# Neighbourhood attention's values with tokens on the partitions, gathered by transfers within SBUF

## The reference, cut to what matters

```python
qa, ka, va, cq, ckv, kr, gates = jnp.split(h @ w_in, IN_SPLITS, axis=-1)
...
v_b = jnp.moveaxis(lax.dynamic_slice_in_dim(vg, rs, kh, axis=1)[:, :, key_col], 2, 1)
...
p = jax.nn.softmax(jnp.concatenate([s_loc, s_ctx], axis=-1), axis=-1).astype(v.dtype)
p_loc = p[..., :n_loc].reshape(B, H, n_blk, NA_QCOLS, kh, NA_KCOLS)
o = (jnp.einsum('bhjqak,bjakhd->bjqhd', p_loc, v_b)
     + jnp.einsum('bhjqk,bkhd->bjqhd', p[..., n_loc:], v_ctx))
```

## Time and profile before

| | before |
|---|---|
| runs shown | 2722.70, 2722.75, 2722.99 us |
| median | 2722.75 us |
| span of the profiled execution | 2720.7 us |
| TensorE busy | 2686.7 us, 99% |
| VectorE, ScalarE, GpSimd busy | 1318.2, 514.4, 822.1 us |
| stretch of the change: end of the rope product to first scores | 816.28 to 823.75 us |

### The profile page before, as it was taken

How to read it: one execution, slowest core, us unless ns; L and a number is a source line. 1 busy time by engine, 2 the same in 40 slices (tenths; PEclk the granted TensorE clock), 3 DMA queues, 4 the chain that set the end, 5 groups by cost and what they waited for, 6 DMA issues and landing times.

```text
span 2720.7 us, 30606 instructions
## 1 busy us (share of the span) xinstructions
PE 2686.7 (99%) x12154; PEld 2037.8 (75%) x12154; DVE 1318.2 (48%) x2572; ACT 514.4 (19%) x1185; POOL 822.1 (30%) x682
## 2 busy tenths in 40 slices
PE   9999999999999999999999999999999999999998
PEld 3655555556886478888888887885578888888887
DVE  7656555577227564334332346217563325544433
ACT  3100000004117361122000102106430011000012
POOL 0433343241313004402443430220044404444420
PEclk9999999999999999999999999999999999999999
DMA  6334333223200102222222221220012222222220
GB/s 259 128 112 139 105 112 124 89 87 126 93 26 17 55 1 78 86 78 83 88 94 79 92 93 62 78 80 32 32 62 84 87 78 93 89 82 93 79 99 31
DMA packets 56926, 231.72 MB, mean 85 GB/s; under 512 B 4432, under 2 KB 16592, under 8 KB 43472
## 3 DMA queue, kind: packets, MB, share of 16 engines
q1 hardware_dynamic: 46112, 194.07, 20.3%
q0 software_dynamic: 8352, 31.46, 3.8%
q10 hardware_dynamic: 2320, 4.24, 0.4%
HBM read 227.66 MB, written 2.10 MB: 84 GB/s over the span
## 4 chain that ended last, share of the span: by engine, by line
PE 61%; DVE 1%; ACT 0%; issue 0%; DVEq 0%; ACTq 0%
PE banks L760 40%; PE banks L675 13%; PE banks L753 2%; PE banks L811 1%; PE banks L1468 1%; PE banks L1387 1%; PE banks L1405 1%; PE banks L922 0%; PE banks L1470 0%; PE banks L1462 0%; PE banks L1315 0%; PE banks L1476 0%; PE banks L1446 0%; PE banks L726 0%; PE banks L727 0%; PE banks L1295 0%
## 5 line engine op out<-in xcount | busy, mean ns | idle before, releaser
L3165 POOL TENSOR_TENSOR big<-weight_ring 128x512 f32<-128x512 f32 (+2 forms) x121 | 146.3, 1209 | 1292.3 <-PE banks L760 674.5
L760 PE MATMUL banks<-big 128*128 128x256 f32 (+1 forms) x2096 | 533.7, 402 | 0.0
L760 PEld LDWEIGHTS banks<-big 128*128 128x128 f32 x2096 | 397.6, 190 | 104.0 <-DVE rpb_rows L2371 2.5
L760 PE MATMUL banks<-big,weight_ring 128*128 128x256 f32 (+1 forms) x1384 | 363.8, 407 | 0.0
L760 PE MATMUL banks<-normed,weight_ring 128*128 128x256 f32 (+1 forms) x1312 | 342.6, 404 | 1.7 <-issue 0.9
L760 PEld LDWEIGHTS banks<-big,weight_ring 128*128 128x128 f32 x1384 | 262.8, 190 | 75.2 <-DVE scratch_b L2377 0.7
L760 PEld LDWEIGHTS banks<-normed,weight_ring 128*128 128x128 f32 x1312 | 249.0, 190 | 68.7 <-issue 1.7
L675 PE MATMUL banks<-normed,weight_ring 128*128 128x256 f32 (+2 forms) x976 | 272.3, 435 | 3.5 <-ACT normed L1627 3.2
L675 PEld LDWEIGHTS banks<-normed,weight_ring 128*128 128x128 f32 (+1 forms) x976 | 180.3, 189 | 74.2 <-issue 50.9
L3166 POOL TENSOR_TENSOR big<-weight_ring 128x512 f32<-128x512 f32 (+2 forms) x146 | 219.1, 1501 | 0.0
L760 PE MATMUL banks<-normed,big 128*128 128x256 f32 (+1 forms) x840 | 203.7, 389 | 0.0
(11 more groups left out here) (503 smaller groups left out, 3443.7 us busy)
## 6 DMA issues: line engine op xcount, KB each, us to landing
weight_ring<-weights SPq DMA_DIRECT2D x144, 1024.0 KB, 4.8
rpb_rows<-w_ada POOLq DMA_DIRECT2D x28, 512.0 KB, 3.9
p_embed<-w_ada POOLq DMA_DIRECT2D x28, 512.0 KB, 3.8
weight_ring<-weights SPq DMA_DIRECT2D x16, 768.0 KB, 4.3
weight_ring<-weights SPq DMA_DIRECT2D x15, 512.0 KB, 3.3
big<-w_ada SPq DMA_DIRECT2D x2, 1536.0 KB, 10.6
residual<-xT SPq DMA_DIRECT2D x3, 1024.0 KB, 15.0
big<-w_ada SPq DMA_DIRECT2D x3, 1024.0 KB, 16.7
```

The lines of the kernel that those rows point to most:

```text
L760: last = nc.tensor.matmul(z, stationary(p), moving(p), start=opens and p == 0, stop=p == kp - 1, skip_group_check=True)
L3165: T(w[2], a11, a21, ALU.subtract).then_inc(sums_c, 1)
```

## The change

Blocks 4 and 5 of the projection are computed with tokens on the partitions, in the form that L753 has, also for the context tokens. The latent tokens go to `V_TOKENS` (the memory of `V_RAW`), the context ones straight to `VN`. From `V_TOKENS` 32 transfers within SBUF, 32 partitions by 512 floats each, bring the window rows to `VN`; ScalarE's queue issues them, in the place where the second eight window copies stood. The window copies, the ten groups of transposes and their ten copies are gone. `VN`, the attention's row buffers and the order of its score banks change places in memory. The squares of `CKV` follow the rope copies at once; their addition stands behind VectorE's second maximum, the two sum products behind the scores of the third pair, the root in ScalarE's loop ahead of the sixth exponential (`i == 5`). GpSimd's first bias rows wait for the transfers instead of for the rope copies, since they overwrite half of `V_TOKENS`; VectorE's first copy of transposed rows and TensorE's first value product wait for the transfers too.

```diff
+TOKENS_OUT = (*V_VM, V_PROJ[4], V_PROJ[5])
...
-NA_S = (0, 1, 6, 7)
+NA_S = (6, 7, 0, 1)
...
+        def proj_part(b, m, l):
+
+            if b in (4, 5):
+                at = (b - 4) * 256 + m * P
+                return V_TOKENS[l][:, :, at:at + P]
+            rows, t = proj_rows(b)
+            return rows[:, t + m, l * HALF:(l + 1) * HALF]
+
+        def window_values(j, r, c):
+
+            at = 64 * (r % 2) + K_START[j]
+            return VN[K_COLS * r:K_COLS * (r + 1), 2 * j + c, :], V_TOKENS[c][at:at + K_COLS, r // 2, :]
...
                 def product(z, stationary, moving, opens, begins=False):
-                    if v in V_VM:
+                    if v in TOKENS_OUT:
...
+                    at = bank[:, 6 + v % 2, w * CTX:(w + 1) * CTX]
                     for k in range(KC):
...
+                        if b in (4, 5):
+                            last = mm(at.rearrange("p (m c) -> p m c", m=2), H[:, k, S + w * P:S + (w + 1) * P],
+                                      slot(PROJ[b]).rearrange("p (m k c) -> p k m c", m=2, c=P)[:, k], k == 0,
+                                      k == KC - 1, w == 0 and k == 0)
...
-            for v in range(10):
-                if v >= 4:
-                    pe.wait_ge(vt["dve"] if v % 2 else vt["act"], (v - 4) // 2 + 1)
-                for c in range(4):
-                    last = nc.tensor.transpose(bank[:, VT_BANK[v % 4], c * P:(c + 1) * P], VA[:, c, v * P:(v + 1) * P], ident)
-                last.then_inc(vt["done"], 1)
-            pe.wait_ge(vt["act"], 5)
-            pe.wait_ge(vt["dve"], 5)
-            pe.wait_ge(lora["sq_used"], QR + 2)
-            nc.tensor.matmul(bank[:, 4, :], ones, SQ[:, 0, 0:S], start=True, stop=True)
-            nc.tensor.matmul(bank[:, 5, 0:CTX], ones, SQ[:, 0, S:T], start=True, stop=True).then_inc(lora["sq_used"], 1)
+
+            def lora_sums():
+
+                pe.wait_ge(proj["act"], 2 + contexts_upto(9) + 1)
+                pe.wait_ge(lora["sq_used"], QR + 2)
+                nc.tensor.matmul(bank[:, 4, :], ones, SQ[:, 0, 0:S], start=True, stop=True)
+                nc.tensor.matmul(bank[:, 5, 0:CTX], ones, SQ[:, 0, S:T], start=True,
+                                 stop=True).then_inc(lora["sq_used"], 1)
...
+                    if w == 2:
+                        lora_sums()
...
                     if w == 3:
                         pe.wait_ge(lora["root"], 3)
+                        pe.wait_ge(vn_landed, 16 * N_WINDOW_LOADS)
...
-                if b in (5, 2):
-                    i = (5, 2).index(b)
+                if b == 2:
                     act.wait_ge(took, 5 * v)
-                    for t in range(2):
-                        for j in range(N_BLK):
-                            A(VA[:, 2 * i + t, j * 256:(j + 1) * 256].rearrange("p (r w) -> p r w", w=K_COLS),
-                              grid_cols(V_RAW[i][:, t, :], K_START[j]), ACT.Copy)
+                    act.wait_ge(c11, copied_upto(v - 1))
+                    for j in range(N_BLK):
+                        for r in range(4):
+                            for c in range(2):
+                                act.dma_start(*window_values(j, r, c)).then_inc(vn_landed, 16)
...
-            for v in range(0, 10, 2):
-                act.wait_ge(vt["done"], v + 1)
-                A(VN[:, v, :], bank[:, VT_BANK[v % 4], :], ACT.Copy).then_inc(vt["act"], 1)
-                if v in (2, 4):
-                    A(SQ[:, v // 2 - 1, :], CKV[:, v // 2 - 1, :], ACT.Square).then_inc(lora["sq"], 1)
-            act.wait_ge(lora["sq_used"], QR + 3)
-            act.wait_ge(lora["normed"], QR)
-            root(lora, BOTH, (4, 5), lora["root"], ML_KV_RANK)
+            act.wait_ge(c11, copied_upto(V_LATER - 1))
+            for k in range(KVR):
+                A(SQ[:, k, :], CKV[:, k, :], ACT.Square).then_inc(lora["sq"], 1)
...
+                if i == 5:
+                    act.wait_ge(lora["sq_used"], QR + 3)
+                    act.wait_ge(lora["normed"], QR)
+                    root(lora, BOTH, (4, 5), lora["root"], ML_KV_RANK)
...
-            for v in range(1, 10, 2):
-                dve.wait_ge(vt["done"], v + 1)
-                V.tensor_copy(VN[:, v, :], bank[:, VT_BANK[v % 4], :]).then_inc(vt["dve"], 1)
...
+                if i == 1:
+                    dve.wait_ge(lora["sq"], QR + KVR)
+                    V.tensor_tensor(SQ[:, 0, :], SQ[:, 0, :], SQ[:, 1, :], ALU.add).then_inc(lora["sq_used"], 1)
...
-            pool.wait_ge(proj["act"], 2 + contexts_upto(9) + 1)
+            pool.wait_ge(vn_landed, 16 * N_WINDOW_LOADS)
             nc.gpsimd.memset(NA_BIAS[:, :, 256:512], 0.0)
```

More of the change, by code:

```diff
@@ L304, in build @@
         KA = view(big, 2048, 4, T)
-        VA = view(big, 5120, 4, N_BLK * 256 + CTX)
-        V_RAW = [view(big, 19712, 2, S), PE2]
+        V_TOKENS = [view(big, 19712, 2, S), PE2]
         CQ = view(big, 10240, QR, S)
@@ L309, in build @@
         KR = big[:, 14848:14848 + T]
-        VN = view(big, 15616, 10, 512)
+        VN = view(big, 5120, 10, 512)
         KM = view(big, 2048, NA_HEADS, T)
@@ L314, in build @@
         VM = view(big, 10240, 6, 512)
-        NA_ROWS = view(big, 5120, 6, 512)
-        NA_TURNED = view(big, 8192, 4, 512)
+        NA_ROWS = view(big, 15616, 6, 512)
+        NA_TURNED = view(big, 18688, 4, 512)
         NA_BIAS = view(p_sb, 0, 2, 512)
@@ L480, in build @@
         proj = st("proj", "done", "act", "dve")
-        vt = st("vt", "done", "act", "dve")
+        vn_landed = sem("window_values_landed")
         ana = st("att_na", "s", "bias", "max", "exp", "inverse", "norm", "t", "tc", "pv", "oc")
@@ L543, in build @@
         NA_SUM = 13 - Q_BANK[3]
-        VT_BANK = (*range(OTHER, OTHER + 3), KR_AT + 2)
+        N_WINDOW_LOADS = 2 * N_BLK * 4
         def proj_rows(b):
@@ L549, in proj_rows @@
                 return KA, 2 * (b - 2)
-            if b < 6:
-                return V_RAW[b - 4], 0
             return (CQ, 2 * (b - 6)) if b < 9 else (CKV, 0)
         def context_rows(b):
+            if 4 <= b < 6:
+                return VN[:, 2 * N_BLK:, (b - 4) * 256:(b - 3) * 256]
             rows, t = proj_rows(b)
-            return VA[:, 2 * (b - 4):2 * (b - 3), N_BLK * 256:] if 4 <= b < 6 else rows[:, t:t + 2, S:T]
+            return rows[:, t:t + 2, S:T]
+        def proj_part(b, m, l):
[7 more added lines that the diff above has]
+            return VN[K_COLS * r:K_COLS * (r + 1), 2 * j + c, :], V_TOKENS[c][at:at + K_COLS, r // 2, :]
         def with_context(b):
@@ L1059, in contexts @@
                 for w in range(2):
+                    at = bank[:, 6 + v % 2, w * CTX:(w + 1) * CTX]
                     for k in range(KC):
-                        last = mm(bank[:, 6 + v % 2, w * CTX:(w + 1) * CTX],
-                                  slot(PROJ[b], (w * KC + k) * P, P), H[:, k, S:T], k == 0, k == KC - 1,
-                                  w == 0 and k == 0)
+                        if b in (4, 5):
+                            last = mm(at.rearrange("p (m c) -> p m c", m=2), H[:, k, S + w * P:S + (w + 1) * P],
+                                      slot(PROJ[b]).rearrange("p (m k c) -> p k m c", m=2, c=P)[:, k], k == 0,
+                                      k == KC - 1, w == 0 and k == 0)
+                        else:
+                            last = mm(at, slot(PROJ[b], (w * KC + k) * P, P), H[:, k, S:T], k == 0, k == KC - 1,
+                                      w == 0 and k == 0)
                 last.then_inc(proj["done"], 1)
@@ L1883, in _ @@
                 v = V_PROJ[b]
-                rows, t = proj_rows(b)
                 if with_context(b):
@@ L1890, in _ @@
                 act.wait_ge(prod, 7 * v + 5)
-                A(rows[:, t, 0:HALF], zones(v)[0], ACT.Copy).then_inc(c11, 1)
+                A(proj_part(b, 0, 0), like(proj_part(b, 0, 0), zones(v)[0]), ACT.Copy).then_inc(c11, 1)
                 if b in (4, 5):
@@ L2773, in _ @@
                 v = V_PROJ[b]
[L2774 to L2777, removed]
+                fast_heads(v, proj_part(b, 1, 1))
+                fast_c21(v, proj_part(b, 1, 0))
+                fast_c12(v, proj_part(b, 0, 1))
                 if b in (4, 5):
@@ L2790, in _ @@
                                                ALU.mult).then_inc(lora["normed"], 1)
-            for v in range(1, 10, 2):
-                dve.wait_ge(vt["done"], v + 1)
-                V.tensor_copy(VN[:, v, :], bank[:, VT_BANK[v % 4], :]).then_inc(vt["dve"], 1)
-                if v == 7:
-                    dve.wait_ge(lora["sq"], QR + KVR)
-                    V.tensor_tensor(SQ[:, 0, :], SQ[:, 0, :], SQ[:, 1, :], ALU.add).then_inc(lora["sq_used"], 1)
             def na_maxima(u):
@@ L2814, in na_turned @@
                     dve.wait_ge(ana["pv"], u // 2 - 1)
+                if u == 0:
+                    dve.wait_ge(vn_landed, 16 * N_WINDOW_LOADS)
                 dve.wait_ge(ana["t"], u + 1)
```

## The result

The changed kernel takes 2732.47 us (median of 5 runs, 2732.05 to 2732.59) against 2722.76 us for the one before (5 runs, 2722.70 to 2723.32): 9.7 us more, ratio 1.0034, 95% interval 1.0023 to 1.0045. Forecast were 2724.5 us and a range up to 2730. The profiled span is 2730.3 us, 9.6 us longer than before, and TensorE's busy time is the same (2686.4 us against 2686.7).

A forecast was written before the change was run, and what follows sets the result against it. TensorE, busy in 2686.7 of 2720.7 us, was taken to bound the kernel. The terms -5.6 + 0.9 + 3.8 + 2.7 summed to +1.8 us, so 2724.5 us, with a range of 2718 to 2730.

The forecast's parts named there:

- The place of the stall: TensorE idles inside block 3's products, before the fourth, for 3.8 us.
- what releases it: VectorE's first addition, which waits for ScalarE's snapshot behind the 32 issues, lets TensorE go on in block 3.
- the formula for it: Block 3 stall is 32p - 9.6 us, with p the us per issue; nothing up to p = 0.30.
- the lower clock behind it: After block 3's stall TensorE runs at its lower clock level for a while, costing 2.7 us.
- the start of the attention: Transposes gone, sums and root moved: 5.6 us won; first scores to sixth pair 14.7 us against 12.9.
- the price of the new product form: Blocks 4 and 5, tokens on partitions: 1.79 us a product instead of 1.73, 0.9 us lost.
- the price of one issue: Each transfer holds ScalarE's queue p = 0.42 us, gap included, between 0.30 and 0.68; stall 3.8 us.
- rival 2: Issues are dear, ScalarE's queue backs up: p 0.54 or more, +5.5 us, at 0.68 2732.9 us; chance 0.18.
- Rival 1: Issues are cheap, p up to 0.38: stall 0 to 2.5 us, clock holds, 2718.0 to 2720.6 us; chance 0.17.
- Rival 3: Transfers land one behind another, bias rows at the attention's start come late: 23 us more, 2748; chance 0.04.
- Rival 4: All 6.0 us and more come back at the attention's start without a stall: faster than 2717.3; chance 0.05.
- Below 2.6 us of stall I count none: In block 3, a stall shorter than 2.6 us was to bring no lower-clock cost.

The follow-up runs named there:

- e3: Changed kernel with its 32 transfers of 64 KB within SBUF as 128 partitions by 128 floats instead of 32 by 512: 2732.36 us, one run.
- e5: Changed kernel with the same bytes in 16 transfers of 64 partitions by 2 KB (128 KB each), issued in the same place: 2719.23 us, one run.
- e4: Changed kernel with its 32 transfers of 32 partitions by 512 floats read from the weights in HBM instead of SBUF: 2727.01 us, one run.
- e1: Changed kernel with the same 32 transfers issued from ScalarE's queue in its four idle gaps: 2718.14 us, ratio 0.9983 to the kernel before.
- e8: Changed kernel with 19 of the 32 issues in their place and 13 behind the snapshot of block 3: 2722.89 us, one run.
- e6: Changed kernel with issues spread over ScalarE's four gaps and the norm's sums back ahead of the first scores: 2722.93 us, ratio 0.9999 to the kernel before.
- e2: Changed kernel with all 32 transfers issued from SyncE's queue, none from ScalarE's: 2718.45 us, ratio 0.9984 to the kernel before.
- e7: Changed kernel with issues spread over ScalarE's four gaps, squares ahead of rope copies and their addition ahead of VectorE's first maximum: 2717.85 us, ratio 0.9979.

## Why the prediction was wrong

**The structure held.** The place of the stall, what releases it, the formula for it, the lower clock behind it, the start of the attention (14.6 us against 14.7) and the price of the new product form (0.8 against 0.9) were all as put. The formula with the measured p gives 32 x 0.647 - 9.6 = 11.1 us, and the stall is 11.1 us; within 0.2 us it also met 16, 19 and the 32 cheaper issues (0.6, 2.6 and 5.7 us of idle time).

**The step that failed** is the price of one issue, "I take 0.42". It was taken between rows of transfers that all had one end in HBM; none had both ends in SBUF, and these cost 0.61 us from ScalarE and 0.59 from SyncE. With the gap, as the prediction counts, p was 0.647. Thirty-two times an error of 0.23 is 7.3 us. With 0.647 in its place the prediction's own sum is -5.6 + 0.9 + 11.1 + 2.7 = +9.1, 2731.8 us. The upper end that the prediction kept, 0.68, did hold the value. The range did not: it cut rival 2 in half, at 2730, and the time fell into the half that was left out with 0.09. The forecast's +1.8 counted as no change, with a chance of 0.73; the measured 9.7 us are clear of noise. (A slip beside it: at p = 0.54 its terms sum to +5.7, not +5.5. It changes nothing here.)

**Rival 2** is what happened, with another cause. It spoke of a queue that backs up. The first issue, with an empty queue, took 0.60 us, and the last 0.61. The first of a row took 0.52 in e3 and 0.53 in e5, so at most 0.1 us of the price can belong to the row. The argument against it, that the issues of 0.68 us moved 1.5 MB each, did not hold either: in the same stretch of the kernel before, an issue of 177.5 KB took 0.67 us, and 128 KB cost the same as 64 in e5.

```profile
2.15 0.67 SPq L624 DMA_DIRECT2D params_sb<-params  x1
```

**Rival 1** fell with the price. The dispatch of about 50 ns in the Trainium skill (DMA: Bandwidth & Descriptors, Anatomy of one DMA) stands there for a transfer that GpSimd issues, and beside a further cost of making the descriptors; it is not the time that an issue holds ScalarE's queue. These issues took twelve times that, and the cheapest of e4, from HBM, 0.32 us.

**Rival 3** fell. Transfers of 64 KB landed 2.0 us after their issue (median), and the last landing let GpSimd go at 799.76, 30 us before the first scores. They lie just at the 64 KB under which the Trainium skill (DMA: Bandwidth & Descriptors, Bandwidth) calls transfers descriptor-dominated. That cost nothing here, since nobody waited for their bandwidth.

**Rival 4** fell too: what the change can bring is e1's 4.8 us, as the sum without a stall had it (4.7).

**The clock.** The price forecast, 2.7 us, was 2.3 in the changed kernel, 2.7 in e4 and 1.8 in e8. That it came so close is partly luck, since the bound beside it, "Below 2.6 us of stall I count none", does not hold. An idle time of 0.60 us in e5 left the clock up and one of 2.60 us in e8 brought it down, but the 2.66 us from which the bound was read were followed by work at the lower clock in three of the ten kernels' traces only (the kernel before, e5, e6); in the other seven work came back at the upper. And about 662 us, ahead of all that was changed, 2.31 us of idle time in e2 were followed by 16 records in 5.41 us where the kernel before took 3.72 behind 2.25 us:

```profile
662.49 5.41 PE L695 MATMUL banks<-normed,weight_ring 128*128 128x256 f32 x16 [2.31 <-ACT normed L1652]
```

```profile
662.02 3.72 PE L675 MATMUL banks<-normed,weight_ring 128*128 128x256 f32 x16 [2.25 <-ACT normed L1627]
```

**Not foreseen** was 1.1 us of lower clock at 1852 us. That it belongs to the level of the clock and not to a new wait is shown by the equal idle times in both traces. Whether it belongs to the change at all is open. It is there in the traces of the changed kernel, e1, e3, e4, e6, e7 and e8, not in those of the kernel before, e2 and e5; each trace is one execution, and the places at 662 us and at the kernel's end differ between traces in the same way although code and idle times there are alike.

## What to carry to other kernels

A transfer that replaces copies costs its issuing queue time, and the instructions behind it in that queue pay: count the issues, multiply by a measured price of the same kind (same pair of memories), and put the row where the engine has nothing due, or on a queue that has nothing due. When the same 32 transfers were spread over idle gaps or moved to SyncE, a loss of 9.7 us became a gain of 4.5 to 4.8. In a kernel that keeps TensorE busy 99% of the time, price a stall with the clock behind it: stalls of 2.6 to 10.9 us in block 3 cost 1.8 to 2.7 us more here. Behind idle times of 1.4 to 2.7 us the clock fell in some traces and not in others, so count its price there as a chance.

## What the runs showed of the hardware

- An issue with both ends in SBUF took 0.61 to 0.62 us from ScalarE, whether 64 or 128 KB, 32, 64 or 128 partitions, and 0.59 from SyncE (64 KB, 32 partitions). The same from ScalarE with its source in HBM took 0.44, SyncE's stores from SBUF to HBM 0.37, its plain weight loads 0.33. Why, these runs don't show.
- Idle times of 1.36 and 0.86 us, a short piece of work apart, left the clock up in one trace and brought it down in another, at a price of 1.1 us. There is a second such place: over 660:668 us the granted clock was 0.79 in e2, e4, e6 and e8, and 1.00 in the other six kernels, though what TensorE does up to there is the same and the idle time 2.25 to 2.40 us in all ten. It cost little: block 4 begins between 717.6 and 718.2 us in all of them.
- The same idle time of 2.66 us at the kernel's end was followed by work at the lower clock in three traces and at the upper in seven.
- A fall of the clock can come after the work is back: in e8 the second product behind the stall was the slower one.
